# Strassen's scheme for the gate and value products of both gated layers of a decoder step

## The reference

```python
def swiglu(u, w_gu, w_down):
    gate, val = jnp.split(u @ w_gu, 2, axis=-1)
    return (jax.nn.silu(gate) * val) @ w_down

h = x + 0.5 * g1 * swiglu(modulate(x, ...), w_ffn1_gu, w_ffn1_down)
...                                   # attention, short convolution, merge, w_out
h = h + 0.5 * g3 * swiglu(modulate(h, ...), w_ffn2_gu, w_ffn2_down)
```

## Time and profile before

| | us |
|---|---|
| median of 3 runs | 1441.39 (1440.62 to 1441.44) |
| the profiled execution itself | 1440.37 |
| its span, first to last instruction | 1438.6 |
| PE busy | 1388.7 (97%) |
| DVE busy | 537.2 (37%) |
| ACT busy | 411.8 (29%) |
| POOL busy | 122.2 (8%) |
| mean granted TensorE clock | 0.985 of full speed |

### The profile page before, as it was taken

One profiled execution on the slowest core, in us unless ns is written; L12 is line 12 of the kernel. 1 busy time (PEld: TensorE's weight loads), 2 busy tenths in 40 slices (PEclk: granted clock), 3 DMA queues, 4 the chain that ended last, 5 costly groups with the idle time before them and its releaser, 6 DMA issues.

```text
span 1438.6 us, 25955 instructions
## 1 busy us (share of the span) xinstructions
PE 1388.7 (97%) x10792; PEld 1284.6 (89%) x10792; DVE 537.2 (37%) x1089; ACT 411.8 (29%) x717; POOL 122.2 (8%) x136
## 2 busy tenths in 40 slices
PE   5899999999999999999999999999999999999996
PEld 1788888999999999999898687799899999999996
DVE  2432322233222125446546545553533333333233
ACT  2512222222211124222225545532522222221111
POOL 3100000000101001000002200034200000001110
PEclk9899999999999999999999999999899999999998
DMA  9457666226333224534472220072122222222331
GB/s 350 154 176 287 215 219 218 87 85 220 90 118 113 68 74 121 169 136 139 150 242 89 87 89 16 23 228 88 54 94 87 87 87 87 87 62 82 90 87 64
DMA packets 97545, 180.56 MB, mean 126 GB/s; under 512 B 13957, under 2 KB 47365, under 8 KB 96430
## 3 DMA queue, kind: packets, MB, share of 16 engines
q1 hardware_dynamic: 97166, 177.17, 37.8%
q10 hardware_dynamic: 288, 2.10, 0.4%
HBM read 173.11 MB, written 10.28 MB: 127 GB/s over the span
## 4 chain that ended last, share of the span: by engine, by line
PE 91%; DVE 3%; SPq 3%; DMA 2%; issue 1%; ACT 1%; POOL 0%; DVEq 0%; POOLq 0%; ACTq 0%
PE PS L1783 66%; PE PS L2079 7%; PE PS L1707 4%; PE PS L1804 3%; PE PS L2093 2%; PE PS L1747 2%; PE PS L2105 2%; PE PS L2121 2%; DMA ada<-in_w_ada 1%; SPq L678 1%; SPq L572 1%; DVE wl L1195 1%; PE PS L2017 0%; PE PS L1764 0%; PE PS L1984 0%
## 5 line engine op out<-in xcount | busy, mean ns | idle before, releaser
L861 ACT ACTIVATE wh<-raw 128x1024 fp32r<-128x1024 f32 (+2 forms) x211 | 200.1, 948 | 788.9 <-PE PS L1783 760.5
L1195 DVE TENSOR_TENSOR wl<-raw,wh 128x1024 fp32r<-128x1024 f32 (+2 forms) x211 | 236.1, 1119 | 503.6 <-ACT wh L861 503.1
L1783 PE MATMUL PS<-uh,wh 128*128 128x272 f32 x1680 | 352.3, 291 | 0.6 <-DVE wl L1195 0.6
L1783 PE MATMUL PS<-uh,wl 128*128 128x272 f32 x1680 | 347.4, 288 | 0.0
L1783 PE MATMUL PS<-ul,wh 128*128 128x272 f32 x1680 | 346.4, 288 | 0.0
L1783 PEld LDWEIGHTS PS<-uh,wh 128*128 128x128 f32 x1680 | 263.6, 188 | 23.6 <-issue 21.7
L1783 PEld LDWEIGHTS PS<-ul,wh 128*128 128x128 f32 x1680 | 264.0, 189 | 0.0
L1783 PEld LDWEIGHTS PS<-uh,wl 128*128 128x128 f32 x1680 | 262.3, 189 | 0.0
L1783 PE MATMUL PS<-hh,wh 128*128 128x272 f32 x704 | 147.2, 290 | 1.8 <-DVE tmp L1310 0.9
L1783 PE MATMUL PS<-hh,wl 128*128 128x272 f32 x704 | 145.7, 288 | 0.0
L1783 PE MATMUL PS<-hl,wh 128*128 128x272 f32 x704 | 145.1, 288 | 0.0
(11 more groups left out here) (269 smaller groups left out, 1448.0 us busy)
## 6 DMA issues: line engine op xcount, KB each, us to landing
raw<-in_w_gu SPq DMA_DIRECT2D x88, 512.0 KB, 3.5
ada<-in_w_ada SPq DMA_DIRECT2D x32, 1024.0 KB, 5.6
raw<-in_w_in SPq DMA_DIRECT2D x39, 512.0 KB, 3.7
raw<-in_w_dn SPq DMA_DIRECT2D x32, 384.0 KB, 3.1
raw<-in_w_dn SPq DMA_DIRECT2D x32, 320.0 KB, 2.9
ch<-in_cmp_pages SPq DMA_DIRECT2D x64, 128.0 KB, 2.3
kv<-in_sel_pages SPq DMA_DIRECT2D x128, 64.0 KB, 1.9
kv<-in_win_tiles SPq DMA_DIRECT2D x16, 256.0 KB, 4.1
```

The costliest lines, as they stand in the source:

```text
L861: e.activation(wh[:, u % SPLITS, 0:n, :], raw[:, u % RAWS, 0:n, :], ACT.Copy).then_inc(hi_ready, 1)
L1195: e.tensor_tensor(wl[:, u % SPLITS, 0:n, :], raw[:, u % RAWS, 0:n, :], f(wh[:, u % SPLITS, 0:n, :]), ALU.subtract).then_inc(lo_ready, 1)
L1783: ins = mm(o[:, a, :], w[:, u % SPLITS, k, :], x[:, k0 + k, HT * a:HT * a + HT], start=(first and k == 0 and w is wh and x is xh), stop=(l ...
```

## The change

Pairs 0 and 1 stay as they are. For pairs 2 to 21 (20 in each layer) gate and value are computed as one 2 x 2 block product: A11 and A12 are the lower and upper four depth tiles of the gate's weights, and for the value the same halves are used plain (A22, the upper) or in sums; the activations' blocks are B11, B12 (lower depth, token half 0 and 1), B21, B22. Seven products of four depth tiles each replace eight. One product is 4 x 3 = 12 matmuls of 272 columns, so a pair has 84. The four weight sums S1 to S4 of a pair (128x512 each) and the four token sums T1 to T4 (128x1088, once a layer) are taken by GpSimd, in float32. ACT rounds and DVE subtracts each of the seven left operands separately, in quarters of `wh`/`wl` (four places of four depth tiles). The products go into three banks; bank 1 is accumulated S2, S3, A22, and DVE reads it in between (U2, U3, C21), bank 2 is accumulated S1, S4 (C22, C12), bank 0 A11, A12 (ACT's copy `sumA`, then the gate's first half). Two sets of three banks alternate.

```diff
-ADA_UNIT, TURN_UNIT = 6, 15
+ADA_UNIT, TURN_UNIT = 8, 17
+A11, S2, S1, S3, A12, A22, S4 = range(7)
+RIGHT = ["B11", "T2", "T1", "T3", "B21", "T4", "B22"]
+PASS_BANK = [0, 1, 2, 1, 0, 1, 2]
+ROUND_AT = {f + 3: [f] for f in range(6)}
+ROUND_AT.update({16: [6, 7], 17: [8, 9], 18: [10, 11], 19: [12]})
...
+            def weight_sum(ug, n, i, j):
+                in0, in1, op = {S1: (v[:, 0:4], v[:, 4:8], ALU.add), S2: (S[:, 0], g[:, 0:4], ALU.subtract),
+                                S3: (g[:, 0:4], v[:, 0:4], ALU.subtract), S4: (g[:, 4:8], S[:, 1], ALU.subtract)}[j]
+                if j == S1:
+                    e.wait_ge(raw_in[(u + 1) % RAWS], 16 * ((u + 1) // RAWS + 1))
...
+                if i:
+                    wait_operand(e, st_lo, lo_ready, ug, n, 7 * (i - 1) + j)
+                e.tensor_tensor(S[:, at], in0, in1, op).then_inc(s_ready, 1)
...
+            def hi(ug, n, i, j):
...
+                else:
+                    wait_operand(e, st_used, unit_used, ug, n, q - 4)
+                ins = e.activation(half_slot(wh, ug, q), operand(ug, i, j), ACT.Copy)
...
+            def strassen(ug, n, i, j):
+                wait_operand(e, st_lo, lo_ready, ug, n, q)
+                for k in range(4):
+                    for w, part in ((wh_, 0), (wh_, 1), (wl_, 0)):
+                        ins = mm(triple(f, PASS_BANK[j]), w[:, k, :], X[:, s, part, k, :],
...
...
+                    strassen(ug, n, i, S1)
+                    e.wait_ge(st_ev, ev + 1)
...
+                    strassen(ug, n, i, S3)
+                    if n == 0:
+                        first_layer(2 * f)
+                    e.wait_ge(st_sum, STEPS * n + i + 1)
+                    strassen(ug, n, i, A12)
+                    e.wait_ge(st_ev, ev + 2)
+                    strassen(ug, n, i, A22)
+                    e.wait_ge(st_ev, ev + 3)
+                    strassen(ug, n, i, S4)
+                    if n == 0:
+                        first_layer(2 * f + 1)
...
             for u in range(4 * KD):
-                if u == 2:
-                    e.wait_ge(ada_used, ADA_GROUPS * KD)
+                if u == 4:
+                    wait_operand(e, st_used, unit_used, U_GU1, 0, 7 * STEPS - 2)
                     pages(0)
```

More of the change, by code:

```diff
@@ L314, in work, with normed, x_set, x_rounded @@
             return (tmp, sg)[k // 2 % 2][:, k % 2, :]
+        def normed(n, k):
+            return work(k) if n == 1 else hx[:, KF - KD + k, :]
+        def x_set(k, a):
+            return SETS[("B11", "B12", "B21", "B22")[2 * (k // 4) + a]]
+        def x_rounded(k, part):
+            s = x_set(k, 0)
+            return X[:, s:s + 5:4, part, k % 4, :]
+        def hidden(fi):
+            if fi < 4:
+                return X[:, SETS["B12"]].rearrange("p h k t -> p (h k t)")[:, T * fi:T * fi + T]
+            if fi < 6:
+                return h_tail[:, fi - 4, :]
+            if fi < 13:
+                return h_ring[:, fi - 6, :]
+            s, at = ("B11", fi - 13) if fi < 17 else ("B21", fi - 16) if fi < 20 else ("B22", fi - 20)
+            return X[:, SETS[s]].rearrange("p h k t -> p (h k t)")[:, T * at:T * at + T]
+        def half_slot(w, ug, q):
+            hs = (q + 2 * (ug % 2)) % 4
+            return w[:, hs // 2, 4 * (hs % 2):4 * (hs % 2) + 4, :]
+        def operand(ug, i, j):
+            u = ug + 2 * (PLAIN + i)
+            if j in (A11, A12, A22):
+                k0 = 0 if j == A11 else 4
+                return raw[:, (u + (j == A22)) % RAWS, k0:k0 + 4, :]
+            return S[:, (S1, S2, S3, S4).index(j)]
+        def triple(f, b):
+            return PS[:, 3 * (f % 2) + b, 0:HT]
+        def piece(buf, x, a):
+            return buf[:, x, HT * a:HT * a + HT]
+        sumA, U2 = piece(tmp, 0, 0), piece(tmp, 0, 1)
+        U3, C22 = piece(tmp, 1, 0), piece(tmp, 1, 1)
+        silu11, silu12 = piece(sg, 0, 0), piece(sg, 0, 1)
+        C21, C12 = piece(sg, 1, 0), piece(sg, 1, 1)
+        def wait_operand(e, part, whole, ug, n, q):
+            i, j = divmod(q, 7)
+            if j == S4:
+                e.wait_ge(whole, ug + 2 * (PLAIN + i) + 2)
+            else:
+                e.wait_ge(part, 6 * STEPS * n + 6 * i + j + 1)
         def mB(m):
@@ new lines, in token_hi, with hidden_hi, second_silu @@
+            def token_hi(n, name):
+                e.wait_ge(t_made, 4 * n + MADE.index(name) + 1)
+                e.activation(X[:, SETS[name], 0], Xf[:, SETS[name], 1], ACT.Copy).then_inc(t_hi, 1)
+            def hidden_hi(fi, og):
+                e.wait_ge(psum_free, og + 2 * fi + 2)
+                e.activation(hidden(fi), hx[:, fi, :], ACT.Copy).then_inc(hid_hi, 1)
+            def second_silu(n, i, f):
+                e.wait_ge(st_ev, 5 * (STEPS * n + i) + 5)
+                e.activation(silu12, C12, ACT.Silu).then_inc(silu_ready, 1)
```

560 lines of the change are left out of this document (376 added, 184 removed).

## The result

| | before | after |
|---|---|---|
| median of the runs, us | 1441.01 (1439.13 to 1441.44) | 1459.86 (1455.57 to 1463.64) |
| ratio after to before | | 1.0134, 95% interval 1.011 to 1.0158 |
| profiled execution / its span, us | 1440.37 / 1438.6 | 1460.39 / 1458.6 |
| mean granted clock of TensorE | 0.985 | 0.976 |

The changed kernel is slower by 18.9 us (20.0 between the two profiled executions); 9.9 were forecast, to 1451.3, in a range from 1408 to 1480. First the page after, against the earlier trace rows: 480 matmuls fewer, TensorE busy 37 us less and in a longer span, DVE from 37 to 57%, POOL from 8 to 26%. In the chain that ended last TensorE falls from 91 to 68%, and DVE stands there with 12%.

What follows compares the result with a forecast made beforehand. TensorE, busy 97% of the span, was taken as the bound. Removal gives 60.2 us, waits give back 70.1: 9.9 slower, 1450.3 on the profiled execution, plus 1.0 for the median, 1451.3 us; range 1408 to 1480.

Steps and rivals of the forecast that it cites:

- The removal: TensorE's gated pairs: 12 matmuls fewer in each of 40 pairs at 0.1254 us, saving 60.2 us.
- U2: DVE's reading before S3, late behind lows and GpSimd sums: 1.15 us in each of 24 pairs, 27.6 us.
- The walk: Timeline of one pair without conditioning steps: U2 ends at 5.55, weights land at 0.3 again, pair takes 11.65 us.
- U3 in two-hidden pairs: Pairs 16 to 18 of both layers, two hidden tiles to subtract: U3 late by 0.9 us, six times, 5.4 us.
- Conditioning: Twelve pairs with two conditioning steps: TensorE waits 1.5 us each for conditioning loads issued late, 18.0 us.
- bias copies: Two bias table copies ahead of U2 in pairs 2 and 3 of the first layer: 1.3 us each, 2.6 us.
- The openings: Start of each gated layer: GpSimd's token sums delay DVE's lows and U2, 7.5 us a layer, 15.0 together.
- The theory's last link: In the openings, token sums of 1088 columns exclude DVE for their whole 2.4 us, which no row showed.
- The end: First down projection: w1 queued behind page transfers lands late; with the gains' placement 1.5 us.
- no exclusion: Rival for DVE and GpSimd: no exclusion worth naming, only conditioning wait and ends remain; 50 us faster, 1391; chance 6%.
- The landing falls elsewhere: Rival for the pairs: weights land later or engines find a fitting phase; 27 us faster, 1414; chance 25%.
- TensorE follows DVE: Rival for the pairs: hand-over delays add up ahead of U2, pair from 12.03; 45 us slower, 1486; chance 24%.

Runs made afterwards that it cites:

- 1: Changed kernel, but GpSimd computes only 8 of the 512 columns of each weight sum from the second pair of a layer on; 1415.98 us, ratio 0.9846.
- 9: Changed kernel, but DVE takes the four weight sums from the second pair of a layer on, its own instructions in the old order; 1417.31 us, ratio 0.9835.
- 10: Changed kernel with U2, C22, conditioning loads and w1 earlier, hidden lows later, openings reordered, and DVE taking weight sums from each layer's second pair; 1393.07 us.
- 11: Against 10, the four token sums and the first pair's weight sums moved to DVE too, so GpSimd takes no sums; 1388.09 us, ratio 0.9637.
- 4: Changed kernel, but SP issues every second conditioning load of the first layer ahead of the same step's weight load; 1441.41 us, ratio 1.0001.
- 12: Against 11, GpSimd adds four 512-column sums a pair into a scratch buffer that nobody reads; 1478.55 us, ratio 1.0269.
- 8: Changed kernel, but GpSimd starts the next pair's sums only after DVE has read U2 of this one; 1476.69 us, ratio 1.0253.
- 3: Changed kernel, but DVE reads U2 ahead of A12's low and C22 directly behind U3, with hidden lows behind U3; 1425.69 us, ratio 0.9886.

## Why the prediction was right, and where it was off

- **The removal**: 60.2 forecast, 57.6 found (40 pairs). A pair went from 12.03 to 10.59 where nothing is late (1, 9, 10): the spacing is 0.1260 (190 us / 1508 in 11), not the 0.1254 that I carried over, and 84 x 0.0006 x 40 is 2 of the 2.6 us. The 116 ns in the prediction is the figure that the Trainium skill's page "TensorE: Matmul & The Clock Gate", section "Back-to-back issue gap", gives for a matmul by itself; where weights are loaded with each matmul, as here, the same section says that both together set the distance.
- **U2** was the right reading, at the right place and for the right reason. The pair: 11.65 forecast, 11.87 found, 1.28 late instead of 1.15. The walk held step by step: with 0 at 1153.93 (the restart of S3 less 1.28 and 36 matmuls) GpSimd begins S1 at 0.44 (0.3), U2 ends at 5.76 (5.55). The landing comes back to the same place each pair.
- **U3 in two-hidden pairs**: 0.9 each forecast; 12.77 less 11.87 is 0.9. Six waits for U3 in the list.
- **Conditioning**: 18.0 forecast; 18.5 came back when the order in SP's queue alone was changed (4).
- **The pairs as a whole**: from U2 to U2 over 19 pairs the first layer takes 268.9 us in the changed kernel and 238.5 in 11, the second 229.0 and 201.0. The first lost 30.4, where my terms for U2, U3, bias copies and conditioning give 30.2; it holds some of the low clock behind the opening, so the agreement is closer than the terms are. The second lost 28.0, not 23.4. Of these 4.6, 2.3 are the 0.13 by which U2 came later in each of 18 pairs, and about 1.7 are the low clock behind the opening's wait, which the forecast put at nothing.
- **The openings**: 7.5 each. In the second layer 405.26 less 371.02 of run 11, less those 28.0: 6.2. The first Strassen pair waits 4.2 for U2 in one layer and 4.4 in the other, as placed. The theory's last link, whether a sum of 1088 columns holds DVE for all its length, is shown: beside T1 and T2 (the two rows of GpSimd) two lows took 5.76 together, where two took 1.36 before. The Trainium skill's page "SBUF — State Buffer", section "Who interferes with whom", says just that of two SBUF inputs, and the trace agrees.

```profile
1043.88 2.54 POOL L916 TENSOR_TENSOR Xf<-hx 128x1088 f32<-128x1088 f32 x1
1046.50 2.90 POOL L916 TENSOR_TENSOR Xf<-hx,Xf 128x1088 f32<-128x1088 f32 x1
1044.23 5.76 DVE L1453 TENSOR_TENSOR X<-hx,X 128x544 fp32r<-128x544 f32 x2 [0.53 <-ACT X L1044]
```

- **The end** is the term that was mis-sized most for its size: 1.5 forecast, 4.4 found in the trace. The products with `w1` were due at about 373 us and came 2.7 late; the issue of the pages ahead of it took 10.3 us, not 8.8. The low clock that followed cost 1.7 more, on which I had nothing.
- 1.6 us lie between the down projection and the second gated layer, where nothing was changed. What they are stays open.
- **Together**: by stretches of the table the forecast was +7.6, +1.5, 0 and +0.8, and +9.0, +4.3, +1.6 and +5.2 were found. The 10.2 us that the sum was short are mostly the pairs of the second layer (4.6), the end (2.8), the removal (2.6) and the open 1.6, less 1.3 for the second opening. The sum is a difference of two larger ones, 70 against 60 us, so small errors of the terms nearly doubled it. The same errors the other way would have left no change at all: the size of the slowing, and even its sign, was less sure than the mechanism.

Of the rivals, *no exclusion* is refuted by 1 and 12. *The landing falls elsewhere* did not happen: the loop stays where it is. A forced other phase (8) is slower as a whole, though for eight pairs it lost only 0.56 each, near the rival's 0.4; an order that comes near 10.6 and lasts was found only when DVE's list was changed too (3, 10.9). *TensorE follows DVE* named the same mechanism with larger losses: 11.87 is nearer to my 11.65 than to its 12.03 and above, and the conditioning wait was 1.5 a pair (18.5 over 12), not 2.8.

What the prediction left out is the better kernel. It counted 7.4 us of DVE work in 10.5 and never asked what four sums would cost there: 4 x 0.61 more is 9.8, which fits, and the exclusion goes. The Trainium skill's page "GPSIMD Engine Reference", section "Engine selection", puts elementwise work with two inputs on VectorE, since GpSimd takes about twice as long; here 1.28 alone on GpSimd against 0.69 on DVE, a factor of 1.9.

## What to carry to other kernels

In these traces, work with two SBUF operands given to an idle GpSimd ran not beside DVE's two-operand instructions but between them. Look for that in the mean of one shape, count such time as DVE's, and try it on DVE where that engine has half as much to spare. When matmuls are taken away, look for the first reading on which TensorE then waits and put it ahead of everything in its engine's list that can wait; and look past the compute engines at each queue whose order was made for the old pace (a load behind another load cost 18 us here). A wait of TensorE can cost more than its own length: look at the granted clock behind it.

## What the runs showed of the hardware that I had not expected

- **A wait can cost twice.** In the changed kernel's second opening, behind a wait of 4.18 us that ends at 1074.60:

```profile
1070.00:1074.60 4.60, 0.42 (x4) 1.00 0.00 0
1074.60:1076.00 1.40, 1.40 (x9) 0.82 0.00 0
1076.00:1078.00 2.00, 2.00 (x11) 0.50 0.51 109
1078.00:1080.00 2.00, 2.00 (x15) 0.77 0.99 389
1080.00:1084.00 4.00, 4.00 (x34) 1.00 0.06 19
```

  That is 0.25 + 1.0 + 0.46 = 1.7 us of matmul time lost beside the wait. The waits of 1.0 to 1.5 in the steady pairs did not lower it (1.00 from 1150 to 1175).
- **The same wait does it or doesn't.** In run 12 each of the pairs shown waits 1.96 us for U3. Behind the wait that ends at 1215.81 the clock is 1.00 and the pair takes 12.81; behind those on either side it falls (0.86 over 12 us) and the pair takes 14.3. In run 8 the clock stayed at 1.00 behind waits of 1.84 that ended at 1101 and 1114 us and was 0.50 two microseconds behind the one that ended at 1140. A rule for it these runs do not give.

```profile
1195.00:1207.00 12.00, 10.04 (x67) 0.86 0.26 87
1207.00:1215.50 8.50, 6.85 (x55) 1.00 0.01 2
1215.50:1220.00 4.50, 4.19 (x33) 1.00 0.70 233
```

- **GpSimd and DVE took turns**, one for one, with work waiting on both: in run 12 each of three DVE instructions in a row took 1.52 to 1.53 beside back-to-back sums.
- **Not only two operands.** In the opening an instruction of DVE with one tensor as operand, 72 columns in SBUF, took 2.30 us beside a sum of 1088 columns that ran from 1052.79 to 1055.79; the same one took 0.20 in the kernel before. The prediction's list of what excludes the sums was too short here; in the steady pair DVE has no such instruction.

```profile
1053.55 2.30 DVE L1374 TENSOR_SCALAR mods<-mods 128x72 f32<-128x72 f32 x1
```
